# Two of 256 row gathers of a PEER feed-forward issued in two parts, 120 tokens and 8 tokens

## The chip, the cores and the metric

The kernel runs on one core of a Trainium2 chip. The metric is the device time of one execution in microseconds (us). Smaller is better. The engines are named as the profile names them: PE (TensorE matmuls), PEld (its weight loads), DVE (VectorE), ACT (ScalarE), POOL (GpSimd) and SP (SyncE, which only issues transfers here). The profile counts 16 DMA engines for the core.

## The reference

Two transformer blocks run one after the other on 256 tokens of width 1024, in float32. The first block is a hybrid of windowed attention and an mLSTM, followed by the part that matters here, a PEER feed-forward:

```
def peer_ffn(x, w_query, sub_keys, expert_down, expert_up):     # blocks of 128 tokens
        q = (xb @ w_query).reshape(t, PEER_HEADS, 2, PEER_KEY_DIM // 2)
        ...
        idx = jnp.take_along_axis(cand_i, best_pos, axis=-1)     # 8 heads x 16 picks for a token
        gate = jax.nn.softmax(best_s, axis=-1)
        u = expert_down[idx]
        act = jax.nn.gelu(jnp.einsum('td,thkd->thk', xb, u).astype(jnp.float32), approximate=False)
        vv = expert_up[idx]
        return jnp.einsum('thk,thkd->td', (gate * act).astype(xb.dtype), vv)
```

Each token picks 128 experts out of 16384, and each expert is a row of 1024 "down" and 1024 "up" numbers. The second block (stick-breaking attention, HGRN2, a gated feed-forward) starts from the sum.

## The kernel before

**Layout.** The host lays the two expert tables side by side, so that `peer_rows` has 16384 rows of 2048 float32 (8 KB). A *pick* is one gather: for one block of 128 tokens, one head and one rank k, it brings one row of `peer_rows` to each of the 128 partitions, 1 MB in all. There are 2 blocks x 8 heads x 16 ranks = 256 picks, numbered p = 0 to 255 and taken in that order. The row numbers stand in `idx`, one column per pick, one token per partition.

**Issue.** POOL issues the picks one by one at L656 as indirect DMAs. They land in `NS` = 14 places (`pick_row(p, ...)`: parts of `rows_w`, `xn` and `arena`); pick p takes place p % 14. From pick 14 on, POOL waits for `row_free` >= p - 13, that is until PE has done with pick p - 14. Each place has a semaphore of its own (`row_sem(p)`), which rises by 16 with each gather, and `landed(p)` is the count at which pick p is complete. The indices come from DVE: it routes two heads at a time, a group ahead, and writes 32 columns of `idx` at L2025 with an increment of `routed`; POOL waits for that at the first pick of every second group of 16.

**Use.** For each pick DVE waits for all of it, multiplies the down half with the token (L2151, one instruction over 128x1024) and leaves a dot product. ACT takes the gelu (L1475), the weight (L1477) and builds a diagonal matrix (L1486). PE multiplies the diagonal with the up half into two banks (L979) and increments `row_free`. The last pick goes another way: DVE adds it to the sum itself (L2173).

**What follows the last pick.** `x3` is complete, PE turns it (L945), multiplies it with the two chunks of the second block's input weights that lie ready in `kept_w` (L968), and goes on with the streamed weights (L699). SP loaded `kept_w` before the picks began and then waits. Its next load, of the streamed weights into `ring`, comes after `row_free` has nearly reached the end and the last two picks have landed:

```
                    for c in range(KEPT):
                        sp.dma_start(kept_w[c], w2[:, :, c * CW:(c + 1) * CW]).then_inc(sem("kept_loaded"), 16)
                    sp.wait_ge(sem("row_free"), 1 + max(last_pick(q) for q in RAW_SLOTS))
                    for p in (PICKS - 2, PICKS - 1):
                        sp.wait_ge(row_sem(p), landed(p))
```

In the listing of the functions that the change touches:

Of the kernel before, what the change touches and what calls it, by code (L numbers as in the profile page):

```python
# [8 lines left out]
U32 = mybir.dt.uint32  # L9
# [5 lines left out]
P = 128  # L15
S = 256
NB = S // P
D = 1024
# [43 lines left out]
CW = 512  # L62
LB = 3
PICKS = NB * PH * TOPK
ARENA_ROWS = 5
NS = ARENA_ROWS + 1 + 8
KEPT = 2
# [22 lines left out]
def build(nc, a, out):  # L90
# [10 lines left out]
    with ctx:  # L101
        def sb(name, shape, dt=F32):
            return ctx.enter_context(nc.sbuf_tensor(name, shape, dt))
# [3 lines left out]
        def sem(name):  # L107
            if name not in made:
                made[name] = ctx.enter_context(nc.semaphore(name))
            return made[name]  # L110
# [137 lines left out]
        n2row = rows_a[:, ARENA_ROWS - 1, 0:D]  # L248
        diag_r = Area(20992).take(NB, P)
        iota16 = sb("iota16", [P, TOPK])  # L250
        dots = sb("dots", [P, 2, TOPK])
        gelu = sb("gelu", [P, 2, TOPK])
        wgt = sb("wgt", [P, 2, TOPK])
# [64 lines left out]
        def pick_row(p, first, n):  # L318

            where, i = PLACES[p % NS]  # L320
            if where == "arena":
                return rows_a[:, i, first:first + n]
            if where == "xn":
                return xn[:].rearrange("p a b -> p (a b)")[:, first:first + n]
            return rows_w[:, i, first:first + n]

        def row_sem(p):
            return sem(f"row{p % NS}")

        def landed(p):  # L330
            return 16 * (p // NS + 1)

        def last_pick(slot):
            return PICKS - 1 - (PICKS - 1 - slot) % NS
# [178 lines left out]
        @block.sync  # L513
        def _(sp):
            for b in range(NB):
                sp.dma_start(xres[:, b, :], a["x"][b * P:(b + 1) * P, :]).then_inc(sem(f"x_loaded{b}"), 16)

            for n, (nm, views) in enumerate(chunks):
                if n == NML:
                    sp.wait_ge(sem("qk_turned"), NB)  # L520
                    sp.wait_ge(sem("ml_qk"), MH // 2)
                    sp.wait_ge(sem("num_evac"), MH)
                    sp.dma_start(sk, a["sub_keys"]).then_inc(sem("sk_loaded"), 16)
                if n == NO1:
                    sp.wait_ge(sem("in_turned"), TURNED_HM + 4)
                    sp.dma_start(n2row, a["n2row"]).then_inc(sem("sk_loaded"), 16)
                if n == NPEER:
                    sp.wait_ge(sem("unit_used"), unit[NO1 - 1, 1] + 2)
                    for c in range(KEPT):
                        sp.dma_start(kept_w[c], w2[:, :, c * CW:(c + 1) * CW]).then_inc(sem("kept_loaded"), 16)  # L530
                    sp.wait_ge(sem("row_free"), 1 + max(last_pick(q) for q in RAW_SLOTS))
                    for p in (PICKS - 2, PICKS - 1):
                        sp.wait_ge(row_sem(p), landed(p))
                for g, v in enumerate(views):
                    m = n - SLOTS
                    if m >= 0 and chunks[m][0] != "query":
                        for half in ((g,) if len(chunks[m][1]) == 2 else (0,)):
                            sp.wait_ge(sem("lo_ready"), unit[m, half] + 2)
                    if nm == "down":
                        to = raw_half(n, g).rearrange("p (r t) c -> p r (t c)", r=2)  # L540
                    elif nm in FLAT:
                        to = raw_half(n, g).rearrange("p t c -> p (t c)").rearrange("p (t c) -> p t c", c=CW)
                    else:
                        to = raw_half(n, g)[:, :, 0:v.shape[2]]
                    if n == 0:
                        m = v.shape[1] // 2
                        sp.dma_start(to[:, 0:m, :], v[:, 0:m, :]).then_inc(sem("unit_loaded"), 16)
                        to, v = to[:, m:, :], v[:, m:, :]
                    sp.dma_start(to, v).then_inc(slot_sem(n, g), 16)
                if n == 1:  # L550
                    for t, v in (("ifbias", ifbias[:]), ("qkgain", qkgain[:]), ("qkcol", qkcol[:]), ("sinks", sinks[:]),
                                 ("mlgain", mlgain[:]), ("sbgain", sbgain[:]), ("hgain", hgain[:]), ("lbt", lbt[:])):
                        sp.dma_start(v, a[t]).then_inc(sem("small_loaded"), 16)
            for b in range(NB):
                for e in range(2):
                    es = slice(e * CW, (e + 1) * CW)
                    sp.wait_ge(sem("x5_ready"), 2 * b + e + 1)
                    sp.dma_start(out[b * P:(b + 1) * P, es], xres[:, b, es]).then_inc(sem("stored"), 16)
            sp.wait_ge(sem("stored"), NB * 2 * 16)

        @block.gpsimd
        def _(pool):
# [75 lines left out]
            for g in range(NB * PH):  # L638
                if g < PR:
                    pool.wait_ge(sem("routed"), 2 * g + 1)  # L640
                elif g % PR == 0:
                    pool.wait_ge(sem("routed"), g // PR + PR + 1)
                for k in range(TOPK):
                    p = g * TOPK + k
                    if p >= NS:
                        pool.wait_ge(sem("row_free"), p - NS + 1)
                    elif p == 4:
                        pool.wait_ge(sem("unit_used"), unit[NQUERY - 1, 1] + 2)
                    elif p == 8:
                        pool.wait_ge(sem("routed"), 2)  # L650
                    elif p == 9:
                        pool.wait_ge(sem("r_ready"), R_X2 + 2)
                    elif p >= 10:
                        pool.wait_ge(sem("query_used"), p - 9)
                    j = g % PH * TOPK + k
                    pool.indirect_dma_start(pick_row(p, 0, 2 * D), None, a["peer_rows"],  # L656
                                            bass.IndirectOffsetOnAxis(ap=idx[:, g // PH, j:j + 1], axis=0)).then_inc(row_sem(p), 16)
            for i, (n, g) in enumerate(halves_of(NPEER, NFFN) + ffn_halves):
# [6 lines left out]
        def _(pe):  # L665
# [292 lines left out]
            def kept_step(b, i):  # L958

                c, t = i // KT, i % KT  # L960
                if i == 0 and b == 0:
                    pe.wait_ge(sem("kept_loaded"), 16 * KEPT)
                    pe.wait_ge(sem("x3p_ready"), KT)
                elif b and c == 0:
                    pe.wait_ge(sem("x3p_ready"), KT + t + 1)
                if b and t == 0:
                    pe.wait_ge(sem("qk2_left"), c + 1)
                ins = pe.matmul(ps[:, c, :], x3p[b][:, t, :], kept_w[c][:, t, :], start=(t == 0), stop=(t == KT - 1))  # L968
                if t == KT - 1:
                    ins.then_inc(sem("qk2_done"), 1)  # L970
# [1444 lines left out]
```

## Time and profile before

| | us |
|---|---|
| median of 3 runs | 1316.33 |
| lowest and highest run | 1314.83, 1317.42 |
| the profiled execution, its own time | 1316.84 |
| its span in the profile | 1315.1 |
| PE busy | 1188.6 (90% of the span) |
| DVE busy | 694.6 (53%) |
| ACT busy | 563.8 (43%) |
| POOL busy | 801.5 (61%) |

The span runs from the first to the last recorded instruction. The profiled execution took 1.7 us more than its span. Times of single rows are us from the start of the span. The busy shares are means over stages that differ: the picks fill the part from about 274 to 920 us, and matrix products with weights that are streamed in fill the rest.

### The profile page before, as it was taken

Reading aid. Unit: us, or ns where it says so; the run is one execution under the profiler, and the core shown is the slowest. Engines: PE = TensorE matmul, PEld = TensorE weight load, DVE = VectorE, ACT = ScalarE, POOL = GpSimd, SP = SyncE. Lnnn points to the kernel's source line nnn. Section 1 sums busy time; section 2 is a strip of 40 time slices with the busy share of each in tenths; the row PEclk is TensorE's granted clock in tenths of the full one; section 3 lists DMA queues with packets and bytes.
Section 4 is the critical chain, followed back from the end, with each engine's and each line's share of the span. In section 5 each row is a group of like instructions: output and inputs, shape, how many; then the busy total and the mean of one; then the engine's idle time right before and its main releaser. Section 6 shows DMA issues by size and latency. Waiting matters only on the chain.

```text
span 1315.1 us, 15916 instructions
## 1 busy us (share of the span) xinstructions
PE 1188.6 (90%) x6024; PEld 839.7 (64%) x6024; DVE 694.6 (53%) x1436; ACT 563.8 (43%) x1259; POOL 801.5 (61%) x493
## 2 busy tenths in 40 slices
PE   8999999997978777877887878898999999999999
PEld 8987999973323333323333333333789999999998
DVE  4443144268677584766758567546589523311111
ACT  7486564323323232234322233223675375544442
POOL 7696568634645544454454445551587469788885
PEclk9999999998999989999899889999999999999999
DMA  8453455679999999999999999998643336455542
GB/s 266 154 161 124 133 177 199 227 316 383 425 425 425 424 426 425 425 424 426 425 425 426 424 425 425 425 425 333 211 159 125 120 125 196 168 188 181 185 160 96
DMA packets 130172, 381.80 MB, mean 290 GB/s; under 512 B 8496, under 2 KB 83248, under 8 KB 97328
## 3 DMA queue, kind: packets, MB, share of 16 engines
q0 software_dynamic: 36864, 268.45, 48.7%
q1 hardware_dynamic: 91760, 112.25, 26.0%
q8 instruction: 47, 0.77, 0.2%
q10 hardware_dynamic: 1472, 0.09, 0.1%
q14 instruction: 29, 0.24, 0.1%
HBM read 379.72 MB, written 1.05 MB: 290 GB/s over the span
## 4 chain that ended last, share of the span: by engine, by line
PE 59%; DMA 31%; DVE 7%; ACT 2%; issue 1%; POOL 1%; SPq 0%; ACTq 0%; DVEq 0%
PE ps L699 30%; DMA rows_w<-peer_rows_in,arena 17%; DMA arena<-peer_rows_in,arena 13%; PE ps L979 7%; PE ps L718 5%; PE ps L1160 4%; DVE rows_w L2151 2%; PE ps L915 2%; PE ps L1113 2%; DVE arena L2151 2%; PE ps L968 1%; PE ps L1062 1%; ACT wgt L1477 1%; ACT diag L1486 1%; DMA ring<-w_in_in 1%
## 5 line engine op out<-in xcount | busy, mean ns | idle before, releaser
L470 POOL TENSOR_TENSOR w_lo<-ring,w_hi 128x1024 fp32r<-128x1024 f32 x190 | 465.6, 2468 | 174.2 <-ACT w_hi L464 174.0
L979 PE MATMUL ps<-rows_w,diag 128*128 128x512 f32 x576 | 276.9, 628 | 53.6 <-ACT diag L1486 53.6
L656 POOL DMA_INDIRECT rows_w<-peer_rows_in,arena x144 | 175.9, 1222 | 157.8 <-PE ps L979 141.0
L464 ACT ACTIVATE w_hi<-ring 128x1024 fp32r<-128x1024 f32 x190 | 195.7, 1058 | 133.5 <-PE ps L699 96.1
L979 PEld LDWEIGHTS ps<-rows_w,diag 128*128 128x128 f32 x576 | 112.3, 200 | 212.0 <-issue 129.7
L2151 DVE CUSTOM_DVE_ANT_0 rows_w<-rows_w,arena 128x1024 f32<-128x1024 f32 x144 | 174.2, 1224 | 111.6 <-DMA rows_w<-peer_rows_in,arena 111.2
L699 PE MATMUL ps<-hT_hi,w_hi 128*128 128x256 f32 x768 | 220.7, 287 | 0.0
L979 PE MATMUL ps<-arena,diag 128*128 128x512 f32 x372 | 182.1, 633 | 40.5 <-ACT diag L1486 40.5
L699 PE MATMUL ps<-hT_lo,w_hi 128*128 128x256 f32 x768 | 218.0, 284 | 0.0
L699 PE MATMUL ps<-hT_hi,w_lo 128*128 128x256 f32 x768 | 217.9, 284 | 0.0
L656 POOL DMA_INDIRECT arena<-peer_rows_in,arena x94 | 117.5, 1250 | 130.2 <-PE ps L979 96.8
L1475 ACT ACTIVATE gelu<-dots 128x4 f32<-128x4 f32 (+2 forms) x74 | 15.2, 205 | 404.0 <-DVE dots L2151 404.0
L979 PEld LDWEIGHTS ps<-arena,diag 128*128 128x128 f32 x372 | 73.7, 203 | 143.9 <-issue 97.3
L699 PEld LDWEIGHTS ps<-hT_hi,w_hi 128*128 128x128 f32 x768 | 147.9, 193 | 2.2 <-issue 0.8
L2151 DVE CUSTOM_DVE_ANT_0 arena<-arena 128x1024 f32<-128x1024 f32 x94 | 113.9, 1223 | 66.8 <-DMA arena<-peer_rows_in,arena 66.5
L699 PEld LDWEIGHTS ps<-hT_lo,w_hi 128*128 128x128 f32 x768 | 148.0, 193 | 0.7 <-issue 0.5
L699 PEld LDWEIGHTS ps<-hT_hi,w_lo 128*128 128x128 f32 x768 | 148.0, 193 | 0.0
L1486 ACT ACTIVATE diag<-ident,wgt 128x128 f32<-128x128 f32 x255 | 83.5, 391 | 10.4 <-PE ps L979 8.0
L979 PE MATMUL ps<-xn,diag 128*128 128x512 f32 x72 | 38.8, 666 | 20.4 <-ACT diag L1486 20.4
L1477 ACT ACTIVATE wgt<-arena,gelu 128x1 f32<-128x1 f32 x256 | 55.5, 283 | 2.4
L2353 DVE TENSOR_TENSOR arena<-ps,arena 128x512 f32<-128x512 f32 x11 | 7.6, 691 | 84.5 <-PE ps L699 80.7
L1160 PE MATMUL ps<-w_hi,arena_r 128*128 128x512 f32 x160 | 50.3, 389 | 0.0
(419 smaller groups left out, 1768.1 us busy)
## 6 DMA issues: line engine op xcount, KB each, us to landing
ring<-w_in_in SPq DMA_DIRECT2D x42, 1024.0 KB, 5.1
ring<-w_ffn_gate_in SPq DMA_DIRECT2D x11, 1024.0 KB, 5.3
ring<-w_ffn_up_in SPq DMA_DIRECT2D x11, 1024.0 KB, 5.3
ring<-w_ffn_down_in SPq DMA_DIRECT2D x11, 1024.0 KB, 4.9
ring<-w_out_in SPq DMA_DIRECT2D x8, 1024.0 KB, 4.9
ring<-w_branch_attn_in SPq DMA_DIRECT2D x4, 1024.0 KB, 5.0
ring<-w_branch_mlstm_in SPq DMA_DIRECT2D x4, 1024.0 KB, 4.9
ring<-peer_w_query_in SPq DMA_DIRECT2D x4, 1024.0 KB, 5.0
```

Of the source, the lines that this page charges most:

```text
L464: act.activation(hi_of(n, u)[:, t, 0:cols], raw_half(n, g)[:, t, 0:cols], ACT.Copy).then_inc(sem("hi_ready"), 1)
L470: pool.tensor_tensor(lo_of(n, u)[:, t, 0:cols], raw_half(n, g)[:, t, 0:cols], hi_of(n, u)[:, t, 0:cols].bitcast(F32), ALU.subtract).then_i ...
L656: pool.indirect_dma_start(pick_row(p, 0, 2 * D), None, a["peer_rows"], bass.IndirectOffsetOnAxis(ap=idx[:, g // PH, j:j + 1], axis=0)).the ...
L699: ins = pe.matmul(to, still, moving, start=(t == 0 and (j == 0 or n == 0) and e == 0), stop=(t == KT - 1 and e == 2), skip_group_check=True)
L718: ins = pe.matmul(banks[j], still, moving, start=(t == 0 and e == 0), stop=(t == KT - 1 and e == 2), skip_group_check=True)
L915: ins = pe.matmul(to, w[:, t, j * P:(j + 1) * P], x3t[:, t, :], start=(t == 0), stop=(t == KT - 1), skip_group_check=True)
L979: ins = pe.matmul(acc[:, c, :], diag[:, p % 4, :], pick_row(p, D + c * CW, CW), start=(p == first), stop=True, skip_group_check=True)
L1113: ins = pe.matmul(to, still, moving, start=(t == 0 and j % 2 == 0 and e == 0), stop=(t == KU - 1 and e == 2), skip_group_check=True)
L1160: ins = pe.matmul(ps[:, 4 + 2 * b + e, :], still, moving, start=(c == 0 and j == 0 and m == 0), stop=False, skip_group_check=True)
L1477: ins = act.activation(wgt[:, o, i:i + 1], gates[:, g * TOPK + i:g * TOPK + i + 1], ACT.Copy, scale=gelu[:, o, i:i + 1])
L1486: act.activation(diag[:, p % 4, :], ident[:], ACT.Copy, scale=wgt[:, o, i:i + 1]).then_inc(sem("diag_ready"), 1)
L2151: dve.tensor_tensor_reduce(row, row, h2[:, g // PH, :], 1.0, 0.0, ALU.mult, ALU.add, dots[:, o, k:k + 1]).then_inc(sem("dot_done"), 1)
```

## The change

Picks 96 and 192 are each gathered by two indirect DMAs in place of one: the first brings the rows of tokens 0 to 119 of the block, the second those of tokens 120 to 127. The indices of the last 8 tokens are first copied by SP from partitions 120 to 127 of `idx` to partitions 0 to 7 of a small new tile, `idx_end`, one column for each of the two picks. POOL waits for that copy between the two parts. Both parts count on the place's own semaphore, so `landed` counts 16 more from such a pick on.

```
+PARTED = (96, 192)
+PART = 120
...
+        idx_end = sb("idx_end", [P - PART, len(PARTED)], U32)
...
         def landed(p):
-            return 16 * (p // NS + 1)
+            return 16 * (p // NS + 1 + len([q for q in PARTED if q <= p and q % NS == p % NS]))
...
                     for c in range(KEPT):
                         sp.dma_start(kept_w[c], w2[:, :, c * CW:(c + 1) * CW]).then_inc(sem("kept_loaded"), 16)
+                    for i, p in enumerate(PARTED):
+                        j = p % (PH * TOPK)
+                        sp.wait_ge(sem("routed"), p // TOPK // PR + PR + 1)
+                        sp.dma_start(idx_end[:, i:i + 1], idx[PART:P, p // (PH * TOPK), j:j + 1]).then_inc(sem("kept_loaded"), 16)
...
+                    if p in PARTED:
+                        i = PARTED.index(p)
+                        pool.indirect_dma_start(pick_row(p, 0, 2 * D)[0:PART], None, a["peer_rows"],
+                                                bass.IndirectOffsetOnAxis(ap=idx[0:PART, g // PH, j:j + 1], axis=0)).then_inc(row_sem(p), 16)
+                        pool.wait_ge(sem("kept_loaded"), 16 * (KEPT + i + 1))
+                        pool.indirect_dma_start(pick_row(p, 0, 2 * D)[PART:P], None, a["peer_rows"],
+                                                bass.IndirectOffsetOnAxis(ap=idx_end[:, i:i + 1], axis=0)).then_inc(row_sem(p), 16)
+                        continue
...
                 if i == 0 and b == 0:
-                    pe.wait_ge(sem("kept_loaded"), 16 * KEPT)
+                    pe.wait_ge(sem("kept_loaded"), 16 * (KEPT + len(PARTED)))
```

## Rows read from the trace of the kernel before

**Rows 1.** The page: what the DMA engines moved, in 40 slices of the span.

```profile
GB/s 266 154 161 124 133 177 199 227 316 383 425 425 425 424 426 425 425 424 426 425 425 426 424 425 425 425 425 333 211 159 125 120 125 196 168 188 181 185 160 96
```

**Rows 2.** The chain that ended last, around the last pick: start, us, what.

```profile
891.42 24.00 DMA arena<-peer_rows_in,arena
915.45 1.22 DVE arena L2151
...
921.94 6.87 PE ps L968 x16
...
929.68 6.87 PE ps L968 x16
936.55 17.27 PE ps L699 x144
```

**Rows 3.** The DMA queues between 276 and 918 us: packets, MB, share of 16 engines.

```profile
q0 software_dynamic: 36864, 268.45, 99.8%
q8 instruction: 9, 0.15, 0.1%
q14 instruction: 16, 0.13, 0.0%
```

**Rows 4.** Busy time by windows: PE, PEld, DVE, ACT, POOL, PEclk, DMA share, GB/s.

```profile
344.00:910.00 566.00, 462.22 (x979) 191.91 (x977) 373.44 (x864) 166.30 (x569) 281.16 (x225) 0.94 1.01 425
...
913.00:913.50 0.50, 0.50 (x2) 0.26 (x3) 0.47 (x1) 0.00 (x0) 0.00 (x0) 1.00 0.20 82
913.50:914.00 0.50, 0.50 (x3) 0.26 (x2) 0.50 (x1) 0.00 (x0) 0.00 (x0) 1.00 0.08 33
914.00:914.50 0.50, 0.50 (x3) 0.06 (x1) 0.50 (x4) 0.20 (x1) 0.00 (x0) 1.00 0.08 33
914.50:915.00 0.50, 0.39 (x1) 0.00 (x0) 0.29 (x2) 0.43 (x3) 0.00 (x0) 1.00 0.04 16
915.00:915.50 0.50, 0.18 (x1) 0.18 (x2) 0.06 (x1) 0.27 (x1) 0.00 (x0) 1.00 0.08 33
915.50:916.00 0.50, 0.50 (x2) 0.26 (x3) 0.50 (x1) 0.00 (x0) 0.00 (x0) 1.00 0.08 33
916.00:916.50 0.50, 0.50 (x3) 0.23 (x2) 0.50 (x1) 0.00 (x0) 0.00 (x0) 1.00 0.04 16
916.50:917.00 0.50, 0.50 (x2) 0.00 (x0) 0.18 (x2) 0.26 (x2) 0.00 (x0) 1.00 0.08 33
917.00:917.50 0.50, 0.30 (x1) 0.00 (x0) 0.00 (x0) 0.47 (x2) 0.00 (x0) 1.00 0.04 16
```

**Rows 5.** Timeline of the last two dot products on DVE, and SP's next load.

```profile
915.45 1.22 DVE L2151 CUSTOM_DVE_ANT_0 arena<-arena 128x1024 f32<-128x1024 f32 x1 [0.66 <-DMA arena<-peer_rows_in,arena]
...
917.86 1.23 DVE L2151 CUSTOM_DVE_ANT_0 arena<-arena 128x1024 f32<-128x1024 f32 x1 [1.19 <-DMA arena<-peer_rows_in,arena]
917.91 22.19 SPq L549 DMA_DIRECT2D ring<-w_in_in  x6
```

**Rows 6.** L656 by windows up to picks 96 and 192: POOL busy, clock, DMA share, GB/s.

```profile
274.00:498.80 224.80, 114.87 (x96) 0.95 0.99 413
274.00:741.90 467.90, 233.83 (x192) 0.93 1.00 419
```

**Rows 7.** Timeline of DVE: the index columns that picks 96 and 192 need.

```profile
486.10 0.18 DVE L2025 CAST arena<-arena 128x32 uint32<-128x32 f32 x1
...
725.40 0.18 DVE L2025 CAST arena<-arena 128x32 uint32<-128x32 f32 x1
```

**Rows 8.** DMA issues: engine, count, KB each, median us to landing.

```profile
arena<-w_in_in SPq DMA_DIRECT2D x1, 2048.0 KB, 14.4
...
ifbias<-ifbias_in SPq DMA_DIRECT2D x1, 8.0 KB, 8.7
```

**Rows 9.** L656 on the page and in the view of the line.

```profile
L656 POOL DMA_INDIRECT rows_w<-peer_rows_in,arena x144 | 175.9, 1222 | 157.8 <-PE ps L979 141.0
...
DMA to landing us min/median/max: 5.9/22.2/25.2
```

## The prediction

> **What bounds the kernel now.** I read the page first, for where the DMA engines are full. From about 330 to 890 us they move 425 GB/s in slice after slice [rows 1]. This is the stage of the picks. Then the chain of waits, to see who sets the pace there and what hangs on its end. The chain goes through a gather that takes 24.00 us from its issue to its landing, then DVE's dot product at 915.45, and after the last pick through work of PE without a gap worth naming: two rounds of products with the kept weights, then the streamed ones [rows 2]. In the windows of this stage PE is busy 462 of 566 us, DVE 373, POOL 281, and the DMA share is 1.01 [rows 4]. So the gathers bound it, and what counts is when the last pick is complete, since PE's work behind it is one chain.
>
> Next I asked what a pick is to the DMA engines. The queue view gives 36864 packets for 256 picks [rows 3], which is 144 for each: 128 rows and one small packet for each of 16 engines. If the rows are shared out evenly, each engine carries 8 rows of a pick. The last two dot products start 2.41 us apart, both after a wait for a gather [rows 5]; over 8 rows that is 0.30 us for a row on one engine. In the full stage the same number comes from 8.19 KB x 16 / 425 GB/s = 0.31 us [rows 4].
>
> Last, the end of the stage in windows of half a microsecond, which decides this case. The share falls to 0.20 in 913.0 to 913.5, and then it is 0.08 or 0.04 up to 917.5, at 33 or 16 GB/s [rows 4]. One row in half a microsecond is 16 GB/s, two are 33. So from 913.5 on I count 2, 2, 1, 2, 2, 1, 2, 1 = 13 rows, 0.30 us apart: the pace of a single engine. One of the 16 engines, call it the last engine, works on alone for 3.6 us (12 rows after the others' last one; 11 to 13 as the window edges fall, 3.3 to 3.9 us). The last pick is complete for DVE at 917.86, and SP's next load goes out at 917.91 [rows 5]. The other engines have been done since about 913.7. What runs alone here costs the whole kernel 3.6 us.
>
> Where this lag is from, the trace shows only in part: instruction packets run on the same engines, 25 of them in this stage, 0.28 MB together [rows 3], worth 34 rows in all. Which engine carries which partitions it doesn't show.
>
> **The change part by part.** *The split itself.* A part of 120 rows is 15 x 8. I assume that it is laid as 8 rows on each of 15 engines and leaves the sixteenth without rows, and that the part of 8 rows is laid as one row on each of 8 engines. Then in the two picks one engine carries 16 rows less, which is 16 x 0.30 = 4.8 us, and up to 8 engines carry 2 rows more, 0.6 us. If the relieved engine is the last one, it ends at 3.6 - 4.8 = -1.2 us against the others, and these now set the end, 0 to 0.6 us later than before. I take 0.3 for that, and 0.1 to 0.2 for the small packets of two more gathers (32 packets; the present ones are already in the pace of 0.30). The gain is 3.6 - 0.3 - 0.15 = 3.15 us, between 3.3 - 0.6 - 0.2 = 2.5 and 3.9. The parted picks lie before the last 63, so all late picks land earlier by then, and DVE waits for the gather at each of the last two [rows 5]: it can follow.
>
> The Trainium skill (DMA: Bandwidth & Descriptors, "Latency and other measured facts") says that engines 7 and 15 are usually slower than the others. It also gives, under "The descriptor swizzle", partitions 124 to 127 to engine 15 in a transfer over 128 partitions. No row here names an engine. By these two statements leaving out the last share would tend to relieve the right one, and the sum would be the one above; they move nothing in it.
>
> *POOL.* Each parted pick costs one more indirect DMA, 1.22 us on POOL [rows 9]. In the stage POOL is busy 281 of 566 us and waits for PE before most issues [rows 4, 9]. A gather is issued 22.2 us before it lands [rows 9], some 9 picks ahead of the engines. So 1.2 us of POOL twice is nothing in time; without that cover it would be 2.4 us.
>
> *The wait on POOL for the copied index.* SP waits for `routed`, copies, and POOL waits for the copy behind the first part. Behind that wait stand all later picks. The columns for pick 96 are written at 486.10 + 0.18, and POOL issues 96 picks before 498.80; those for pick 192 at 725.40, with 192 picks before 741.90 [rows 6, 7]. That leaves 12.5 and 16.3 us for the copy of 32 bytes. No copy inside SBUF beside full engines is in the trace. The nearest rows: 8 KB landed in 8.7 us behind bigger loads, 2 MB in 14.4 [rows 8]. So the wait is 0 by the one and up to 2 us by the other; I take 0. Even 2 us would be covered by the 22.2 us that are queued on the engines. The engines would starve, and time would be lost one for one, only from a landing of about 12.5 + 20 = 32 us on. Bounds: 0 and 0.
>
> *SP and PE.* SP does nothing between its loads of `kept_w` and 917.91 [rows 5], so its two new waits and copies hold up nobody: routing for pick 192 is done near 726. PE's raised wait on `kept_loaded` comes at pick 206, behind the copy that POOL has needed for pick 192: 0. DVE, ACT and the arithmetic stay as they are: 0.
>
> *Sum.* Against the profiled execution: span 1315.1 - 3.15 = 1311.95, with the 1.7 us around it 1313.7. This execution is 0.5 us above the median, so against the median: 1316.33 - 3.15 = 1313.2 us. A change of 0.2% (2.6 us) is about what a measurement of this kernel can tell from none; the forecast is 0.24%.
>
> **The rivals.**
>
> *The relief falls on another engine.* The last engine is not the one that is left out. For it: nothing in the rows ties the lag to the last 8 tokens, and instruction packets, 25 of them, may land anywhere [rows 3]. Against it: the lag is one engine's alone, 3.6 us beside a spread of the others that ends together, and every pick lays the same partitions on the same engines, so a lasting cause would be the same each time. The end stays where it is, or the last engine gets the 2 further rows: 1316.3 to 1316.9 us. This is also the rival that the change doesn't do what it says.
>
> *The shares turn.* If each gather that does not fill 16 engines moves the starting engine on for the next, 15 engines take the first part and the 8 rows begin on the one left out: it saves 7 rows, not 8. Pick 192 then leaves out another engine. The last engine saves 7 x 0.30 = 2.1 us: 1314.2 us, no change that can be told. The rows show only gathers of 128, which can't tell this. The Trainium skill (DMA: Bandwidth & Descriptors, "Why a DMA increments its semaphore by 16 and not by 1") has this rule: the largest number of engines up to 16 that divides the partition count, taken from a round-robin cursor. It names as an exception some direct copies that always deal shares over all 16, which would be the assumption of my sum. No row here shows which holds for a gather.
>
> *Rows pile up on the last engine (the other side).* The part of 8 rows is not spread, but goes whole to one engine, as 8 rows of one share do now. If in both picks that is the last engine, and it also has its 8 rows of the first part, it carries 16 rows more: +4.8 us, 1321.1 us. It decides from 9 further rows on that engine on (9 x 0.30 = 2.7 us). If it falls on another engine, that one ends at -1 to 0 + 4.8 us against the others' end, some 0 to 1 us behind today's end. For it: today 8 rows of a pick are one engine's share [rows 3]. Against it: it must hit the same engine in both picks, and that must be the late one.
>
> *POOL's wait starves the engines.* It needs 32 us for 32 bytes, against 14.4 for 2 MB [rows 8]. From there each us counts; at 40 us the two would give 16 us, 1332. I give it 2 in 100.
>
> **How the numbers follow.** Relief as assumed 0.50 (of it 0.42 above 0.2%), the relief on another engine 0.24, shares that turn 0.12 (of it 0.02 above 0.2%), rows that pile up 0.08, POOL's wait 0.02, none of these 0.04. The likeliest is the first: 1313.2 us. Faster by over 0.2%: 0.42 + 0.02 = 0.44. Slower by over 0.2%: 0.08 + 0.02 and 0.03 of the rest = 0.13. Within 0.2%: 0.43. The range leaves out the piled rows, the starved engines and the edges: from 1316.33 - 3.9 - 0.2 = 1312.2 to 1316.9 + 0.4 = 1317.3, where 0.2 and 0.4 stand for the scatter of the median. The likeliest case by itself reaches from 1312.2 to 1314.0.
>
> **What the profile after would show.** Right: the tail in which one engine works alone is gone or under 1 us; the last pick lands 2.5 to 3.9 us earlier, near 914.7, and the whole chain behind it by the same; the middle of the stage is at 425 GB/s as before; pick 96 and pick 192 have two rows on L656's successors, and POOL's wait between them is under 2 us. Wrong: the tail of 33 and 16 GB/s is still 13 rows long (relief elsewhere), about 6 rows long (shares turn), or longer than 13 (piled up); a hole in the DMA share near 520 or 765 us would be POOL's wait. The prediction also fails if the last engine's lag is not a steady property of the kernel, but comes out differently in each execution.

## The result, and the profile after

The changed kernel takes 1330.72 us (median of 4 runs, 1330.09 to 1331.45) against 1316.88 us for the kernel before (4 runs, 1314.83 to 1318.20). The ratio is 1.0106, with a 95% interval from 1.0093 to 1.0118: 13.8 us slower. The profiled execution took 1330.09 us, its span is 1328.4 us against 1315.1. The forecast was 1313.2 us.

In the changed kernel POOL's L665 is the first part, L668 the second and L671 the old L656; DVE's L2166 is the old L2151, PE's L994 the old L979.

The page first, with the rows that answer to [rows 1] and to the queue of [rows 3], the latter here for the whole span.

```profile
GB/s 267 150 159 127 142 161 206 246 317 390 425 425 424 425 425 364 425 425 426 425 425 426 385 390 425 426 425 334 191 159 127 128 128 191 164 190 186 189 159 95
...
q0 software_dynamic: 36928, 268.45, 49.1%
```

The stage that was flat at 425 GB/s has two dips now, in the slice from 498 us and in the two from 731 us, just where picks 96 and 192 are worked off. The gathers move the same bytes in 64 more packets. So nothing more is moved; it moves more slowly in two places.

Busy time by windows (the columns are those of [rows 4]): around the two dips, and the whole stretch.

```profile
517.00:526.00 9.00, 3.25 (x8) 1.14 (x6) 2.92 (x7) 0.99 (x5) 3.53 (x4) 0.80 1.01 218
758.00:769.00 11.00, 7.39 (x18) 3.04 (x16) 3.19 (x5) 0.98 (x4) 5.25 (x6) 0.96 1.01 211
500.00:530.00 30.00, 19.25 (x36) 8.08 (x37) 12.17 (x23) 7.00 (x27) 11.38 (x10) 0.82 1.02 358
740.00:780.00 40.00, 28.77 (x57) 12.13 (x56) 16.73 (x31) 7.00 (x27) 15.53 (x14) 0.79 1.01 362
344.00:910.00 566.00, 450.31 (x953) 187.22 (x953) 364.65 (x847) 161.24 (x551) 280.07 (x227) 0.93 1.01 417
```

The last two columns are what counts. For 9 and 11 us the DMA share is 1.01 and the rate 218 and 211 GB/s: all 16 engines are busy, and each row takes twice its 0.30 us. An idle engine would have lowered the share; it did not fall. The time lost is (425 - 358)/425 x 30 = 4.7 us in the first place and (425 - 362)/425 x 40 = 5.9 us in the second. The row of the whole stretch gives the same sum: (425 - 417)/425 x 566 = 10.7 us.

POOL's timeline at pick 96: start, duration, what, and the idle time before it.

```profile
498.79 0.98 POOL L665 DMA_INDIRECT rows_w<-peer_rows_in,arena  x1 [0.99 <-PE ps L994]
500.07 1.31 POOL L668 DMA_INDIRECT rows_w<-peer_rows_in,idx_end  x1 [0.30 <-issue]
501.68 0.96 POOL L671 DMA_INDIRECT rows_w<-peer_rows_in,arena  x1 [0.31 <-issue]
```

POOL didn't wait for the copied index: the 0.30 us before the second part is what also stands before the pick behind it (0.31). At pick 192 it is 0.30 us too.

DVE's timeline where these rows land, around pick 96 and then around pick 192. The line with `idx_end` is the parted pick.

```profile
518.22 1.23 DVE L2166 CUSTOM_DVE_ANT_0 rows_w<-rows_w,arena 128x1024 f32<-128x1024 f32 x1 [1.81 <-DMA rows_w<-peer_rows_in,arena]
...
523.71 1.23 DVE L2166 CUSTOM_DVE_ANT_0 rows_w<-rows_w,arena 128x1024 f32<-128x1024 f32 x1 [4.26 <-DMA rows_w<-peer_rows_in,arena]
...
528.73 1.23 DVE L2166 CUSTOM_DVE_ANT_0 rows_w<-rows_w,arena 128x1024 f32<-128x1024 f32 x1 [3.26 <-DMA rows_w<-peer_rows_in,idx_end]
```
```profile
762.43 1.23 DVE L2166 CUSTOM_DVE_ANT_0 rows_w<-rows_w,arena 128x1024 f32<-128x1024 f32 x1 [3.42 <-DMA rows_w<-peer_rows_in,arena]
...
768.06 1.22 DVE L2166 CUSTOM_DVE_ANT_0 xn<-xn,arena 128x1024 f32<-128x1024 f32 x1 [4.39 <-DMA xn<-peer_rows_in,arena]
...
771.01 1.23 DVE L2166 CUSTOM_DVE_ANT_0 arena<-arena 128x1024 f32<-128x1024 f32 x1 [1.72 <-DMA arena<-peer_rows_in,arena]
...
775.69 1.23 DVE L2166 CUSTOM_DVE_ANT_0 rows_w<-rows_w,arena 128x1024 f32<-128x1024 f32 x1 [2.65 <-DMA rows_w<-peer_rows_in,idx_end]
```

At pick 96 two picks are late, the parted one (528.73) and the whole one in front of it (523.71): each comes 5.0 to 5.5 us after the one before, where the pace was 2.4 us. At pick 192 the dot product before these lines started at 757.78, so the three whole picks in front come after 4.7, 5.6 and 3.0 us, and the parted one after 4.7. The neighbours pay as well. It will matter below.

The end of the stage, in windows of half a microsecond, and SP's next load. This answers to [rows 4, 5].

```profile
923.50:924.00 0.50, 0.36 (x1) 0.30 (x2) 0.21 (x1) 0.09 (x1) 0.00 (x0) 1.00 0.15 66
924.00:924.50 0.50, 0.50 (x2) 0.19 (x1) 0.50 (x1) 0.00 (x0) 0.00 (x0) 1.00 0.08 33
924.50:925.00 0.50, 0.50 (x2) 0.19 (x1) 0.50 (x3) 0.00 (x0) 0.00 (x0) 1.00 0.12 49
...
930.00:930.50 0.50, 0.49 (x2) 0.00 (x0) 0.00 (x0) 0.43 (x3) 0.00 (x0) 1.00 0.08 33
930.50:931.00 0.50, 0.06 (x1) 0.07 (x1) 0.00 (x0) 0.38 (x1) 0.00 (x0) 1.00 0.00 0
```
```profile
931.13 5.41 SPq L556 DMA_DIRECT2D ring<-w_in_in  x4
```

One engine still works on alone, and for longer: from about 924.2 to 930.5 us, 6.3 us or some 21 rows at 0.30 us (an estimate of its start: the windows from 924.0 on hold 23 rows, so one or two are still another engine's), where it was 13 rows before. SP's load goes out at 931.13 instead of 917.91, which is 13.2 us later. Of these, 10.6 to 10.7 us were lost in the two dips and the other 2.6 us are the longer end (by the windows 6.3 us less the 4.0 us of 13 rows, 2.3 us). The span grew by 13.3 us, so everything behind the picks has just moved back with them.

### The profile page after: what moved, and what is told of

Read it like the earlier page. It is cut to its first block, busy times and chain, and to the rows that moved or that the text cites. A ratio compares the mean times of both kernels' runs of the same rounds, so it can differ in the third digit from the quotient of the medians.

```text
span 1328.4 us, 15920 instructions
## 1 busy us (share of the span) xinstructions
PE 1188.4 (89%) x6024; PEld 839.2 (63%) x6024; DVE 695.2 (52%) x1436; ACT 563.8 (42%) x1259; POOL 802.1 (60%) x495
## 4 chain that ended last, share of the span: by engine, by line
PE 58%; DMA 31%; DVE 7%; ACT 2%; issue 1%; POOL 0%; ACTq 0%; DVEq 0%
PE ps L714 30%; DMA rows_w<-peer_rows_in,arena 18%; DMA arena<-peer_rows_in,arena 13%; PE ps L994 7%; PE ps L733 5%; PE ps L1175 4%; DVE rows_w L2166 2%; PE ps L930 2%; PE ps L1128 2%; DVE arena L2166 2%; PE ps L983 1%; PE ps L1077 1%; ACT wgt L1492 1%; ACT diag L1501 1%; PE ps L800 0%
## 5 line engine op out<-in xcount | busy, mean ns | idle before, releaser
L994 PE MATMUL ps<-rows_w,diag 128*128 128x512 f32 x576 | 277.5, 629 | 72.8 <-ACT diag L1501 72.8
L671 POOL DMA_INDIRECT rows_w<-peer_rows_in,arena x142 | 170.8, 1203 | 174.2 <-PE ps L994 156.8
L994 PEld LDWEIGHTS ps<-rows_w,diag 128*128 128x128 f32 x576 | 112.1, 199 | 232.3 <-issue 130.0
L2166 DVE CUSTOM_DVE_ANT_0 rows_w<-rows_w,arena 128x1024 f32<-128x1024 f32 x144 | 174.2, 1224 | 121.0 <-DMA rows_w<-peer_rows_in,arena 114.7
L994 PE MATMUL ps<-arena,diag 128*128 128x512 f32 x372 | 180.9, 629 | 35.7 <-ACT diag L1501 35.7
L671 POOL DMA_INDIRECT arena<-peer_rows_in,arena x94 | 120.0, 1277 | 124.4 <-PE ps L994 92.6
L994 PEld LDWEIGHTS ps<-arena,diag 128*128 128x128 f32 x372 | 73.8, 203 | 138.5 <-issue 97.0
L2166 DVE CUSTOM_DVE_ANT_0 arena<-arena 128x1024 f32<-128x1024 f32 x94 | 113.9, 1224 | 67.3 <-DMA arena<-peer_rows_in,arena 67.1
L994 PE MATMUL ps<-xn,diag 128*128 128x512 f32 x72 | 39.2, 671 | 19.0 <-ACT diag L1501 19.0
```

The costliest lines, as they stand in the source:

```text
L994: ins = pe.matmul(acc[:, c, :], diag[:, p % 4, :], pick_row(p, D + c * CW, CW), start=(p == first), stop=True, skip_group_check=True)
L2166: dve.tensor_tensor_reduce(row, row, h2[:, g // PH, :], 1.0, 0.0, ALU.mult, ALU.add, dots[:, o, k:k + 1]).then_inc(sem("dot_done"), 1)
```

## The experiments

Each kernel was timed beside the kernel before on its own chip, and the chips differ: the kernel before has a median of 1324.75 us beside the first four, 1322.95 beside the next four, 1316.58 and 1316.69 us beside the last two pairs. Only ratios are compared across them. The loss of a place is worked out as above from the rate in the windows 505 to 560 and 750 to 800 us of the profiled execution; in these windows the changed kernel itself has 388 and 375 GB/s, or 4.8 and 5.9 us. Experiments 9 and 10 are edits of the kernel before, the others of the changed kernel. The edits are cut to their main lines; where a pick has one gather only, `landed` counts 16 for it again.

**1. The copy and the wait alone.** The gathers are whole again; SP's copies and POOL's waits stay.

```
                     if p in PARTED:
                         i = PARTED.index(p)
-                        pool.indirect_dma_start(pick_row(p, 0, 2 * D)[0:PART], ...)
                         pool.wait_ge(sem("kept_loaded"), 16 * (KEPT + i + 1))
-                        pool.indirect_dma_start(pick_row(p, 0, 2 * D)[PART:P], ...)
-                        continue
                     pool.indirect_dma_start(pick_row(p, 0, 2 * D), ...)
```

> All 256 picks are gathered whole; only SP's two copies of 8 indices and POOL's two waits for them stay. Theory A (the slow rows belong to the gather of 120 rows) and theory B (to the parting itself, two gathers into one place): no loss, 1317 us plus or minus 1.5, no stretch below 420 GB/s near 520 and 765 us. Rival C (the copy beside full engines, or the wait on it, slows or stalls the engines): the 13 us of the changed kernel stay, near 1330 us.

Measured: 1323.9 us, ratio 0.9993 (0.9981 to 1.0004). Windows:

```profile
505.00:560.00 55.00, 42.66 (x87) 17.69 (x87) 35.78 (x94) 13.80 (x53) 26.49 (x23) 0.92 1.01 425
750.00:800.00 50.00, 40.86 (x79) 16.70 (x78) 34.33 (x94) 15.78 (x61) 22.44 (x21) 0.86 1.01 425
```

Both places run at 425 GB/s. The copy and its wait cost nothing; the loss is in the gathers.

**2. The first part alone.** The rows of tokens 120 to 127 of picks 96 and 192 are left out.

```
-                        pool.indirect_dma_start(pick_row(p, 0, 2 * D)[PART:P], ...)
```

> Picks 96 and 192 gather tokens 0 to 119 alone; the rows of tokens 120 to 127 are left out in these two picks and the places keep what stood there. Theory A (the gather of 120 rows is laid out so that rows take twice as long): both half-rate stretches of some 9 us stay and the time is 1327 to 1331 us. Theory B (the second gather, of 8 rows, or two gathers on one place): no half-rate stretch, 1313 to 1318 us. In both the tail tells whether the last engine was relieved: under 1 us if it was, 3.6 us or more if not.

Measured: 1337.62 us, ratio 1.0106 (1.0068 to 1.0143).

```profile
505.00:560.00 55.00, 42.70 (x86) 17.52 (x85) 30.92 (x78) 11.67 (x45) 24.26 (x22) 0.91 1.01 391
750.00:800.00 50.00, 32.61 (x70) 13.24 (x68) 25.11 (x60) 13.45 (x52) 19.80 (x19) 0.93 1.01 373
```

Lost are 4.4 and 6.1 us, as much as with the second part. So the gather of 120 rows does it by itself, and the 8 rows, small as they are, add nothing that shows.

**3 and 4. Other sizes: 112 and 16, 64 and 64.** Each of these numbers can be shared out over 16 engines, 120 can't.

```
-PART = 120
+PART = 112      # the other kernel: 64
```

> The same parting with 112 and 16 tokens, which are 7 and 1 rows on each of 16 engines. Theory A1 (120 rows use 15 engines, and it is the odd number that costs): no half-rate stretch, 1316 to 1319 us, tail as before at 3.6 us. Theory A2 (any gather that does not span the 128 partitions is laid on the engines in other blocks of partitions than a whole one, and rows collide where they are written): half-rate stretches stay, 1324 to 1332 us.

> The same parting in the middle, 64 and 64 tokens: 4 rows on each of 16 engines twice. Theory A1 (the number 15): no loss, 1316 to 1319 us. Theory A2 (a part that spans only some partitions is written through fewer ways): two half-rate stretches, as long or longer than those of 120 and 8, 1324 to 1335 us. If the 64 rows go to 8 engines with 8 rows each, the two parts together load 8 engines twice and the loss is also there, but only on these.

Measured: 1334.99 us, ratio 1.0076 (1.0049 to 1.0104), and 1335.54 us, ratio 1.0091 (1.0063 to 1.0118). The windows of 112 and 16, then those of 64 and 64:

```profile
505.00:560.00 55.00, 43.93 (x86) 18.06 (x85) 30.00 (x78) 11.72 (x45) 24.11 (x22) 0.87 1.01 390
750.00:800.00 50.00, 35.55 (x73) 14.38 (x71) 26.82 (x71) 14.79 (x58) 23.36 (x20) 0.93 1.01 388
```
```profile
505.00:560.00 55.00, 39.52 (x77) 16.64 (x78) 30.04 (x76) 11.66 (x45) 22.30 (x20) 0.84 1.01 384
750.00:800.00 50.00, 34.25 (x68) 13.78 (x66) 26.25 (x71) 14.82 (x59) 20.93 (x19) 0.86 1.01 383
```

The loss is 4.5 and 4.4 us, and 5.3 and 4.9 us. It is not tied to 15 engines: it also comes when all 16 have the same number of rows. Both kernels post 32 packets more than before, one per engine for each further gather; the changed kernel posts 64 more. These are (16 + 8 + 8) x 2: for the part of 120 one engine has no rows and 8 small packets, for the part of 8 rows 8 engines have none and one small packet each. The sharing that the prediction assumed fits that count.

**5. Four parted picks in a row.** Picks 96 to 99 are parted at 120, with one copy of four columns.

```
-PARTED = (96, 192)
+PARTED = (96, 97, 98, 99)
...
-                        sp.dma_start(idx_end[:, i:i + 1], idx[PART:P, p // (PH * TOPK), j:j + 1])...
+                    sp.dma_start(idx_end[:], idx[PART:P, PARTED[0] // (PH * TOPK), j:j + len(PARTED)])...
```

> Picks 96, 97, 98 and 99 are parted in 120 and 8, one behind the other, in place of 96 and 192; one copy brings their indices. So far each parted pick costs 4.5 to 5.3 us of the engines' time, in a stretch of 9 to 11 us at half the rate, which is more than the 120 rows of one pick explain: at 26 rows in a us half the rate over 9 us is some 235 rows. Theory A2 (the rows of a part collide with each other): each parted pick has its own slow stretch, 36 us of half rate or more in all, 18 to 21 us lost against before. Theory A3 (the part is laid otherwise than whole picks, and its rows collide with those of the whole picks before and behind it, on engines that are some us apart): only the two seams cost, 5 to 8 us lost, and the rate between them is near 425 GB/s.

Measured: 1334.88 us, ratio 1.0089 (1.006 to 1.0119).

```profile
505.00:560.00 55.00, 32.96 (x59) 13.68 (x60) 22.86 (x56) 9.34 (x36) 19.97 (x19) 0.75 1.02 319
750.00:800.00 50.00, 38.25 (x89) 16.21 (x88) 28.84 (x68) 15.74 (x63) 25.31 (x22) 0.97 1.01 425
```

The four lose (425 - 319)/425 x 55 = 13.7 us; one alone lost 4.7 us. Neither a pure cost per pick (18.8 us) nor a pure cost of the seam (4.7 us) is near, and both forecasts failed. The ratio is worth 11.8 us (7.9 to 15.7). Two parts fit, one per parted pick and one per place: (13.7 - 4.7)/3 = 3.0 us for each pick, and 4.7 - 3.0 = 1.7 us for the seam between parted and whole gathers. This is an estimate: two terms from two measurements. With the 5.9 us of the second place the split would be 2.6 and 3.3 us.

**6. The first 64 rows alone.** As experiment 4, and tokens 64 to 127 of picks 96 and 192 are left out.

> Picks 96 and 192 gather tokens 0 to 63 alone, the rows of the other 64 tokens are left out. Theory A2: the loss goes with the rows in the part, half of that of 64 and 64, about 2.5 us each; the 64 rows that are not fetched save 1.2 us each, so 1325 to 1329 us by this chip's 1324.75 of before. Theory A3 (the seam costs, not the rows): 4 us each less 1.2, 1329 to 1332 us.

Measured: 1330.04 us, ratio 1.0059 (1.0031 to 1.0088).

```profile
505.00:560.00 55.00, 40.60 (x80) 16.60 (x80) 32.12 (x83) 12.45 (x50) 23.47 (x20) 0.88 1.01 394
750.00:800.00 50.00, 39.95 (x76) 16.54 (x77) 29.74 (x77) 14.99 (x58) 21.97 (x19) 0.86 1.01 396
```

Lost are 4.0 and 3.4 us, so the second 64 rows of experiment 4 account for 1.3 and 1.5 us. That fits 4 rows on each engine at about twice 0.30 us each (4 x 0.30 = 1.2 us more). The rest, 1.9 to 2.7 us, would be the seam. The runs spread widely here, from 1327.4 to 1333.1 us.

**7. Parts of 124 and 4.** It asks how the rows are dealt.

```
-PART = 120
+PART = 124
```

> The same parting with 124 and 4 tokens. If rows are dealt out in equal shares over the largest number of engines up to 16 that divides them, 124 rows go to 4 engines with 31 rows each, 9.5 us of work on these at full rate: a gap of 7 us between them and the others, in each parted pick, 1335 to 1345 us on the last chip's 1324.75. If they are dealt as 8 to each engine and 4 to the last, the time is that of 120 and 8, some 13 us above before (1337), and the small packets per parted pick are 16 + 4 and 16 + 12.

Measured: 1347.13 us, ratio 1.0182 (1.0152 to 1.0211). The queue of the gathers on the page, DVE's start on pick 96, and windows: the first place, and the end of the stage.

```profile
q0 software_dynamic: 37664, 268.46, 49.3%
```
```profile
545.88 1.23 DVE L2166 CUSTOM_DVE_ANT_0 rows_w<-rows_w,arena 128x1024 f32<-128x1024 f32 x1 [17.32 <-DMA rows_w<-peer_rows_in,idx_end]
```
```profile
520.00:545.00 25.00, 14.39 (x28) 5.77 (x26) 4.06 (x9) 2.33 (x9) 8.64 (x8) 0.79 1.02 246
526.00:545.00 19.00, 9.43 (x16) 3.86 (x16) 1.69 (x5) 2.33 (x9) 3.92 (x5) 0.72 1.01 233
935.00:936.00 1.00, 0.41 (x2) 0.29 (x2) 0.22 (x1) 0.63 (x2) 0.00 (x0) 1.00 0.57 238
...
937.00:938.00 1.00, 0.69 (x2) 0.00 (x0) 0.54 (x4) 0.89 (x3) 0.00 (x0) 1.00 0.47 197
...
940.00:941.00 1.00, 0.53 (x2) 0.30 (x2) 0.32 (x1) 0.44 (x2) 0.00 (x0) 1.00 0.46 197
```

There are 800 packets more than before, 400 for each parted pick: 16 for the second gather, 12 x 31 + 12 x 1 = 384 small ones. So 124 rows went as 31 to each of 4 engines, and 12 engines had none. That is the largest number up to 16 that divides 124. The end of the stage shows how many engines were loaded: a share of about 0.5 for 6 us, so 8 of the 16 are late. Had both picks loaded the same 4 engines, the share would be 0.25. So the shares turn from one such gather to the next. This agrees with what the Trainium skill says (DMA: Bandwidth & Descriptors, "Why a DMA increments its semaphore by 16 and not by 1"), which the prediction left open for a gather.

The time is some 24 us above the kernel before, where at most about 20 were expected: the 31 rows were priced at full rate. Pick 96 is complete for DVE 19.1 us after the pick in front of it (526.80), which is 31 rows at 0.62 us. And the window from 526 to 545 us shows something that the other runs can't: 233 GB/s for 19 us are some 540 rows. At 0.30 us a row the 12 engines that have no row of the first part would alone have moved 12 x 19 / 0.30 = 760. If the four engines did only their 124 rows in it, the twelve moved 416, which is 35 each or 0.55 us a row, with the share at 1.01. A parted gather slows engines that carry none of its rows.

**8. Only the last pick parted.**

```
-PARTED = (96, 192)
+PARTED = (255,)
```

> Only pick 255, the last, is parted in 120 and 8. Nothing comes behind it. Theory A2 (own rows collide): its own 120 rows take twice as long on every engine, 2.4 us more at the end, also on the last engine: +2 to +3 us. Theory A3 (seams): one seam of two, +0 to +3 us, since most engines have time to spare at the end while the last engine meets no one. If the engine that gets no rows were the last one, the end would come 2.4 us earlier: -2.4 us.

Measured: 1329.66 us, ratio 1.0055 (1.0022 to 1.0087). DVE's last dot products, and a window before the end:

```profile
918.67 1.23 DVE L2166 CUSTOM_DVE_ANT_0 rows_w<-rows_w,arena 128x1024 f32<-128x1024 f32 x1 [0.72 <-DMA rows_w<-peer_rows_in,arena]
...
922.56 1.23 DVE L2166 CUSTOM_DVE_ANT_0 arena<-arena 128x1024 f32<-128x1024 f32 x1 [2.13 <-DMA arena<-peer_rows_in,arena]
...
927.00 1.23 DVE L2166 CUSTOM_DVE_ANT_0 arena<-arena 128x1024 f32<-128x1024 f32 x1 [2.68 <-DMA arena<-peer_rows_in,arena]
...
930.46 1.23 DVE L2166 CUSTOM_DVE_ANT_0 arena<-arena 128x1024 f32<-128x1024 f32 x1 [1.71 <-DMA arena<-peer_rows_in,arena]
...
933.07 1.23 DVE L2166 CUSTOM_DVE_ANT_0 arena<-arena 128x1024 f32<-128x1024 f32 x1 [1.38 <-DMA arena<-peer_rows_in,idx_end]
```
```profile
921.00:922.00 1.00, 1.00 (x3) 0.52 (x4) 0.00 (x0) 0.00 (x0) 0.00 (x0) 1.00 1.08 172
```

It cost more than the 0 to 3 us that were expected: the ratio is worth 7.3 us (2.9 to 11.5). From 918.67 to 933.07 the last four picks take 14.4 us, where four at 2.41 us take 9.6. The picks 252, 253 and 254 in front of the parted one, whole gathers, come 1.5, 2.0 and 1.1 us late, the parted one only 0.2. A likely reason, not shown by itself: the engines that are ahead are already on the parted pick's rows and slow down the whole ones of the engines behind (172 GB/s with a full share from 921 to 922 us). The 4.8 us are close to the 4.7 of the first place. The early part of this profiled execution also ran otherwise than [rows 4], so its absolute times don't compare.

**9. The same two picks parted by columns.** Each is two gathers of half a row (4 KB) for all 128 tokens; DVE writes the doubled indices.

```
+                    if p in HALVED:
+                        for c in range(2):
+                            pool.indirect_dma_start(pick_row(p, c * D, D), None, a["peer_rows"].rearrange("r (c d) -> (r c) d", c=2),
+                                bass.IndirectOffsetOnAxis(ap=idx_half[:, HALVED.index(p), c:c + 1], axis=0)).then_inc(row_sem(p), 16)
```

> Picks 96 and 192 are each issued as two gathers again, but cut by columns: all 128 tokens' down halves, then all 128 tokens' up halves, 4 KB rows from the same table read as 32768 rows of 1024; DVE writes 2 x index and 2 x index + 1 for the two picks. Both parts span the 128 partitions. Theory A (the cost is in parts that span fewer partitions, laid on the engines otherwise than a whole pick): no half-rate stretch, -1 to +1 us against before. Theory B (two gathers for one pick cost as such): stretches of half rate as in the changed kernel, +10 to +13 us.

Measured: 1317.13 us, ratio 1.0006 (0.9996 to 1.0015).

```profile
505.00:560.00 55.00, 44.96 (x91) 18.63 (x92) 36.48 (x96) 12.35 (x48) 25.87 (x23) 0.91 1.01 424
750.00:800.00 50.00, 39.07 (x79) 16.13 (x78) 35.10 (x96) 15.89 (x61) 25.41 (x20) 0.90 1.01 424
```

No dip. Two gathers for one pick are harmless here, where each spans the 128 partitions.

**10. Columns, for the last two picks.** To bring work forward at the end: the halves that the dot products need first, the halves for the sum last.

```
+                    if p in HALVED:        # picks 254 and 255
+                        pool.indirect_dma_start(pick_row(p, 0, D), None, half_rows, ...).then_inc(row_sem(p), 16)
+                        if p == PICKS - 1:
+                            pool.wait_ge(sem("row_free"), PICKS - 12)
+                            for i, q in enumerate(HALVED):
+                                pool.indirect_dma_start(pick_row(q, D, D), None, half_rows, ...).then_inc(row_sem(q - 12), 16)
```

> Only the last two picks are cut by columns: down half of 254, down half of 255, then the up halves of 254 and 255. All else is as before. If gathers that span 128 partitions keep the full rate, the two last dot products start 1.2 to 2.4 us earlier, while the last up half lands as before; the weight of the last pick is ready by then, and DVE adds the last pick some 0.1 us after its landing in place of 1.96 us: 1.2 to 1.9 us faster (0.1%). If the cut costs a seam of 2 us, no gain or a loss of 1 to 3 us.

Measured: 1316.57 us, ratio 1.0001 (0.9992 to 1.001).

```profile
913.46 1.23 DVE L2170 CUSTOM_DVE_ANT_0 arena<-arena 128x1024 f32<-128x1024 f32 x1 [0.66 <-DMA arena<-peer_rows_in,arena]
...
915.13 1.21 DVE L2170 CUSTOM_DVE_ANT_0 arena<-arena 128x1024 f32<-128x1024 f32 x1
...
916.27 1.22 DVE L2170 CUSTOM_DVE_ANT_0 arena<-arena 128x1024 f32<-128x1024 f32 x1
...
919.54 1.41 DVE L2193 SCALAR_TENSOR_TENSOR xres<-arena,wgt,ps 128x512 f32<-128x512 f32 x2 [2.04 <-PE ps L993]
```

The same sum in the kernel before:

```profile
919.82 1.41 DVE L2173 SCALAR_TENSOR_TENSOR xres<-arena,wgt,ps 128x512 f32<-128x512 f32 x2 [0.72 <-PE ps L979]
```

The last dot product starts 1.6 us earlier than in [rows 5] and waits for no DMA. But pick 253 still lands only for 913.46, and the last sum waits for PE's products of the picks before, 2.04 us now and 0.72 us before. It starts 0.3 us earlier, and nothing was gained. The kernel before already had this wait: its chain runs through the dot product of pick 254 at 915.45 [rows 2] and PE, not through the landing of the last pick.

**11 and 12. Sixty-four rows in the middle, sixty-four at the top.** Experiments 2 to 9 leave two readings: any gather over fewer than 128 partitions is slow, or it depends on which partitions are written together. Only 64 rows of picks 96 and 192 are gathered, from copied indices.

```
+PART = 64
+START = 32       # the other kernel: 64
...
-                        pool.indirect_dma_start(pick_row(p, 0, 2 * D)[0:PART], ... ap=idx[0:PART, g // PH, j:j + 1], ...)
-                        pool.indirect_dma_start(pick_row(p, 0, 2 * D)[PART:P], ...
+                        pool.indirect_dma_start(pick_row(p, 0, 2 * D)[START:START + PART], ...
                                                 bass.IndirectOffsetOnAxis(ap=idx_end[:, i:i + 1], axis=0)).then_inc(row_sem(p), 16)
```

> Picks 96 and 192 are gathered only for tokens 32 to 95, from indices that SP copied to partitions 0 to 63; the rows of the other 64 tokens of these two picks are left out, so 1.05 MB less is moved, which is 2.5 us at 425 GB/s. The control is the kernel in which only tokens 0 to 63 were left in: 394 and 396 GB/s in the windows 505 to 560 and 750 to 800, 4.0 and 3.4 us lost. Theory P (the lost time depends on which partitions the rows of a gather go to, because rows that are written at the same time meet at the same place of SBUF): partitions 32 to 95 lie half in the lower 64 and half in the upper, and the loss falls away: 420 GB/s or more in both windows, 0 to 1 us lost in each, ratio to before about 0.998. Theory N (any gather that spans fewer than 128 partitions runs at half the rate, wherever they lie): 390 to 398 GB/s in both windows as in the control, ratio about 1.006. The Trainium skill (SBUF - State Buffer, Door 1: The DMA port swizzle) gives partitions 0 to 63 eight of the sixteen ports and its table gives partitions 32 to 95 all sixteen; by it Theory P holds.

> The same as the kernel with tokens 32 to 95, with tokens 64 to 127 in their place: only these are gathered in picks 96 and 192, from copied indices; the other 64 rows are left out. Both theories expect the half rate here, since these partitions are the upper half alone: 390 to 398 GB/s in the windows 505 to 560 and 750 to 800, 3.4 to 4.5 us lost in each, ratio to before about 1.006. If it runs at 420 GB/s or more, the loss of the kernel with tokens 0 to 63 is tied to those partitions or to indices used in place, and not to half of the partitions.

Measured: 1314.44 us, ratio 0.9985 (0.9975 to 0.9994), with partitions 32 to 95; 1323.78 us, ratio 1.0054 (1.0037 to 1.0071), with 64 to 127. The windows, first those with 32 to 95, then those with 64 to 127:

```profile
505.00:560.00 55.00, 42.39 (x92) 17.34 (x91) 38.48 (x102) 11.87 (x46) 27.87 (x24) 0.97 1.01 425
750.00:800.00 50.00, 39.47 (x81) 16.32 (x82) 36.82 (x101) 17.64 (x69) 24.75 (x21) 0.93 1.01 425
```
```profile
505.00:560.00 55.00, 42.45 (x87) 17.53 (x86) 33.74 (x92) 11.67 (x45) 23.50 (x21) 0.88 1.01 393
750.00:800.00 50.00, 38.54 (x80) 15.87 (x80) 31.46 (x88) 15.77 (x61) 20.85 (x20) 0.90 1.01 398
```

The two kernels differ in one number, the first partition. With 32 to 95 there is no dip at all, seam included, and the time falls by 2.3 us, about the 2.5 us that the left-out rows take at 425 GB/s. With 64 to 127 the loss is 4.1 and 3.2 us, that of experiment 6. So the count of partitions is not the cause; which partitions are written together is. Nor is it what is read: the rows of tokens 32 to 63 came slowly in experiment 6 and those of 64 to 95 in experiment 12, and here both come at full rate.

## Why the prediction was wrong

**The step that failed** is the cost of a row. The sum priced every row at 0.30 us "on one engine", a figure of whole picks, and asked only how many rows each engine gets. The rate of an engine in [rows 4] is that of whole gathers over 128 partitions, and it didn't carry over. A term was missing: what is lost while a gather over part of the partitions is worked off beside them. It measured 4.7 and 5.9 us at the two places of the changed kernel, 10.6 us in all; experiment 5 divides the first into some 3.0 us for the pick and 1.7 us for the seam. The prediction's bounds for an operation that the trace doesn't show, 0 to 0.2 us for "small packets", covered its packets and not its rate. The gain that the sum put against this, 3.6 us less of one engine working alone at the end, did not come either: that end grew by 2.6 us.

**What meets where.** The runs show that 64 rows cost nothing in partitions 32 to 95 and 3.2 to 4.1 us, besides their own 1.2 us, in 0 to 63 or 64 to 127. The Trainium skill names the place (SBUF — State Buffer, "Door 1: The DMA port swizzle"): the partitions hang on 16 ports, 0 to 63 reach eight of them, 64 to 127 the other eight, and by its table 32 to 95 reach all sixteen. Experiments 6, 11 and 12 agree, with 394, 425 and 393 GB/s in the window from 505 us. For 120 rows the same table gives an estimate: if each of 15 engines takes 8 neighbouring partitions in order and in step, they stand at any time on 8 ports, two engines to a port, and the 8 rows of each take 8 x 0.30 = 2.4 us more, against 3.0 measured. That the shares are neighbouring partitions is inferred; no run shows it. The Trainium skill (DMA: Bandwidth & Descriptors, "The descriptor swizzle") also has each engine write one port of its own in a transfer over 128 partitions; that would explain why whole picks run at 425 GB/s whatever lead one engine has. And it would explain in part, though no run isolates it, why neighbours pay: an engine on a parted pick writes to ports that belong to others, which are still on a whole one. It doesn't explain how far this goes.

**How far it goes.** In experiment 7 four engines carry the part of 124 rows and the other twelve are at half pace too, for 19 us. A reading that fits, argued and not tested: as long as any engine has rows of a gather that is slow in this way, all are at half pace. For 124 rows that is 31 x 0.62 = 19 us, of which half is lost, 9.6 us against (425 - 246)/425 x 25 = 10.5 measured. For 120 rows the 9 to 11 us of half rate would be 8 x 0.62 = 5 us, and 4 to 6 us by which the first engine leads the last (the one late engine before is 3.6 us behind the others). Half of that lead, 2 to 3 us, would be the seam.

**The relief did not reach the end.** The part of 120 rows does leave one engine without rows (64 packets), as assumed. That this engine is the last one was a guess. The shares turn, as far as parts of 124 rows show it (experiment 7), and then the two picks relieve two different engines: the rival to which I gave 0.12, right in its mechanism. Its price of 2.1 us saved did not come, since one engine worked alone for 6.3 us instead of about 4. Why this end grew by 2.6 us isn't settled: the slowed rows may fall unevenly on the engines, but which engine is last, and with which rows, was not measured. With equal shares and no dip (experiment 11) a single engine also works alone, from about 911.5 to 915 us, so the end lag belongs to the kernel. It isn't of one size, which the prediction named as a way to fail: counted as in [rows 4] it is 10 rows in experiment 1 and 13 in experiment 9, whose gathers all span 128 partitions, 19 in experiment 3, 13 in experiment 12 and 21 in experiment 8.

**What was right.** POOL's further issues cost nothing, nor did the copy and its wait (0.9993 in experiment 1, 0.30 us on POOL), those on SP and PE included; the rate away from the two places stayed at 425 GB/s; and all behind the last pick moved one for one with it (13.2 us of 13.3). The list of signs of failure named a hole in the DMA share. The loss showed as a hole in the rate with the share full. "None of these" had 4 in 100: the rivals asked which engine gets the rows, none what the rows meet.

**No better version.** Of the kernels that compute the whole reference, parting by columns was level (1.0006 and 1.0001), and every parting by partitions was slower.

## What to carry to other kernels

A gather into part of the partitions can run at half the rate though every DMA engine is busy, and it slows the whole gathers beside it; read the GB/s beside the share. What cost nothing here was 64 partitions half in the lower and half in the upper 64 (32 to 95), and a cut by columns over all 128. The pace of an engine taken from one shape of transfer is not its pace for another: bound it by what else could be shared, not only by the packets. Before aiming at the one engine that ends last, find out whether it is the same one each time, and what comes next in line: here bringing the last dot product forward by 1.6 us moved the sum behind it by 0.3 us, since that waited for PE.

## What the runs showed of the hardware

- 64 rows of 8 KB written to partitions 0 to 63 or 64 to 127 beside whole gathers cost 3.2 to 4.1 us; written to partitions 32 to 95 they cost nothing (425 GB/s).
- A gather's rows are dealt to the largest number of engines up to 16 that divides them: 124 rows went to 4 engines, and parting two picks so cost 1.0182. Each engine without rows adds one small packet for every row that one of the others carries (800 packets more with 124 and 4), and the next such gather begins on other engines.
- One pick parted at 120 costs 4.7 to 5.9 us, and one to three whole picks in front of it are late with it. While 4 engines work off 124 rows, all 16 are at half pace: 233 GB/s at a share of 1.01 for 19 us.
